# Two gate gemms, two norms and a split of the first block made one stage, with compact roots and output weights fetched ahead

## The reference, cut to what matters

```python
def rms_norm(t, w, groups):
    tg = t.reshape(t.shape[:-1] + (groups, t.shape[-1] // groups))
    tg = tg * lax.rsqrt(jnp.square(tg).mean(-1, keepdims=True) + EPS)
    return tg.reshape(t.shape) * w

def merge(s, y, o):   # z and g are columns of h @ w_in
    ys  = rms_norm(y * silu(s['z']), ssd_nw, 2)          # SSD_GROUPS = 2
    os_ = rms_norm(o, hg_nw, 8) * silu(s['g'])           # HG_HEADS = 8
    return jnp.concatenate([ys, os_], axis=-1) @ w_out
```

## Time and profile before

| | |
|---|---|
| runs | 3270.03, 3287.79, 3285.07 us |
| median | 3285.07 us |
| profiled execution, its own time | 3267.99 us |
| its span, first to last instruction | 3266.2 us |
| mean granted TensorE clock | 0.896 |
| TensorE (matmul) busy | 2748.4 us, 84% |
| VectorE busy | 1703.7 us, 52% |
| ScalarE busy | 1079.5 us, 33% |

### The profile page before, as it was taken

How to read it: one execution, slowest core, us unless ns; L and a number is a source line. 1 busy time by engine, 2 the same in 40 slices (tenths; PEclk the granted TensorE clock), 3 DMA queues, 4 the chain that set the end, 5 groups by cost and what they waited for, 6 DMA issues and landing times. The chain is left out here.

```text
span 3266.2 us, 41926 instructions
## 1 busy us (share of the span) xinstructions
PE 2748.4 (84%) x15966; PEld 2125.7 (65%) x15966; DVE 1703.7 (52%) x2643; ACT 1079.5 (33%) x1788; POOL 91.9 (3%) x101
## 2 busy tenths in 40 slices
PE   7979899756658999998968999957799847599998
PEld 4634887645346788786637888846666636478886
DVE  3535222677554588637976877342224362454432
ACT  3322101354212555324334554221124210245531
POOL 0034000000000000000000000000000000000000
PEclk9989999966878999999988999978769967699999
DMA  8723132001014233421112333222100100223332
GB/s 294 248 81 129 52 84 58 13 4 47 7 52 135 65 97 96 112 62 52 51 30 61 102 97 95 80 58 76 52 7 1 47 1 2 65 78 96 96 98 71
DMA packets 374147, 240.99 MB, mean 74 GB/s; under 512 B 8048, under 2 KB 345840, under 8 KB 374000
## 3 DMA queue, kind: packets, MB, share of 16 engines
q1 hardware_dynamic: 374000, 238.96, 24.6%
HBM read 236.31 MB, written 2.10 MB: 73 GB/s over the span
## 5 line engine op out<-in xcount | busy, mean ns | idle before, releaser
L1086 DVE SCALAR_TENSOR_TENSOR ffn_acc<-ffn_pad,cols_sb,ffn_acc 128x512 f32<-128x512 f32 x380 | 263.7, 746 | 32.6 <-ACT ffn_acc L1013 32.6
L223 PE MATMUL bank<-ffn_x_high,pre_high 128*128 128x512 f32 x528 | 212.2, 402 | 14.2 <-DVE ffn_x_low L475 10.7
L224 PE MATMUL bank<-ffn_x_low,pre_high 128*128 128x512 f32 x528 | 210.6, 399 | 0.0
L225 PE MATMUL bank<-ffn_x_high,pre_low 128*128 128x512 f32 x528 | 210.6, 399 | 0.0
L223 PE MATMUL bank<-ffn_x_high,ffn_w_high 128*128 128x512 f32 x528 | 205.5, 389 | 0.0
L225 PE MATMUL bank<-ffn_x_high,ffn_w_low 128*128 128x512 f32 x528 | 205.5, 389 | 0.0
L224 PE MATMUL bank<-ffn_x_low,ffn_w_high 128*128 128x512 f32 x528 | 205.4, 389 | 0.0
L223 PE MATMUL bank<-ffn_h_high,ffn_down_w_high 128*128 128x512 f32 x480 | 190.3, 397 | 0.0
L224 PE MATMUL bank<-ffn_h_low,ffn_down_w_high 128*128 128x512 f32 x480 | 189.6, 395 | 0.0
L225 PE MATMUL bank<-ffn_h_high,ffn_down_w_low 128*128 128x512 f32 x480 | 188.7, 393 | 0.0
L1307 DVE SCALAR_TENSOR_TENSOR conf_u<-conf_pad,cols_sb,conf_u 128x512 f32<-128x512 f32 x162 | 121.8, 752 | 16.9 <-ACT conf_u L1274 11.7
(11 more groups left out here) (734 smaller groups left out, 6388.0 us busy)
## 6 DMA issues: line engine op xcount, KB each, us to landing
ada_ring<-in_ada_w SPq DMA_DIRECT2D x48, 1024.0 KB, 7.0
pre_ring<-in_ffn_w_up SPq DMA_DIRECT2D x88, 512.0 KB, 3.9
pre_ring<-in_ffn_w_in SPq DMA_DIRECT2D x44, 512.0 KB, 3.9
ffn_down_ring<-in_ffn_w_down SPq DMA_DIRECT2D x28, 704.0 KB, 4.7
ffn_down_ring<-in_ffn_w_out SPq DMA_DIRECT2D x14, 704.0 KB, 4.5
pre_ring<-in_conf_w SPq DMA_DIRECT2D x18, 512.0 KB, 5.0
f_ring<-in_mix_w_in SPq DMA_DIRECT2D x32, 256.0 KB, 3.0
mix_out_ring<-in_mix_w_out SPq DMA_DIRECT2D x16, 512.0 KB, 3.9
```

Source lines behind the costliest of these rows:

```text
L223: pe.matmul(bank, weights[0], acts[0], start=start, stop=False)
L224: pe.matmul(bank, weights[0], acts[1], start=False, stop=False)
L225: return pe.matmul(bank, weights[1], acts[0], start=False, stop=stop)
L1086: dve.scalar_tensor_tensor(out=dst, in0=src, scalar=conv_w(2 * i + j, n), in1=dst, op0=ALU.mult, op1=ALU.add).then_inc(tapped[j], 1)
```

## The change

`gate_by`, `group_norm` and the call of `split` go. In their place stands one stage, `branch_gates`, that runs 16 gate tiles one after the other: tiles 0 to 7 are z's, tiles 8 to 15 are g's.

- Weight slabs come whole into the two slots of `pre_ring` and are split into `pre_high` and `pre_low` by ScalarE (`take_high`) and VectorE (`take_low`). Two more slabs, 16 and 17, are the weights of the output gemm's first tile; `closing` is told with `ahead=2 * DT` to take them from there.
- `o` is squared and counted ahead of the first product; `y` is squared and counted tile by tile. Roots are taken of 128 x 32 values (all of `o`) and 128 x 4 (a group of `y`) and spread over banks 5 and 6: for `o` two tiles at a time behind products 2 to 5, for the groups of `y` behind products 7 and 11.
- From tile 8 on VectorE forms `y` times gain and root, and `y` and the gated `o` are split in the same stage.

The diff, cut to its core:

```diff
-def gate_by(core, name, y, w_gate, x, sq=None):
...
-def group_norm(core, y, sq, groups, gain, square):
...
+def branch_gates(core, w_z, w_g, w_out, x, y, o, y_parts, o_parts):
...
+        o_counts, y_counts = banks[4], [banks[7], banks[4]]
...
+        def stage_at(s, shift=0):
+
+            return {1: 0, 6: 1, 10: 2}.get(s - shift)
+
+        @block.sync
+        def _(sp):
+            for s in range(slabs + 2):
+                if s >= 2:
+                    sp.wait_ge(low_done, s - 1)
+                sp.dma_start(ring[:, s % 2], slab(s)).then_inc(slab_in[s % 2], 16)
+
+        @block.tensor
+        def _(pe):
+            def product(s):
+                pe.wait_ge(low_done, s + 1)
+                if s >= 4:
+                    pe.wait_ge(gate_done, s - 3)
...
+            def o_root_out(k):
+                pe.wait_ge(inverted, 1)
+                if k >= 2:
+                    pe.wait_ge(o_scaled, k - 1)
+                spread_tokens(banks[5 + k % 2], lambda t: o_root[:, k * TT + t:k * TT + t + 1]).then_inc(o_spread, 1)
+
+            def y_root_out(n):
+                pe.wait_ge(inverted, n + 2)
+                pe.wait_ge(o_scaled, DT)
+                spread_tokens(banks[5 + n], lambda t: y_root[:, n, t:t + 1]).then_inc(y_spread, 1)
+
+            for k in range(DT):
+                o_count(k)
+            for s in range(slabs):
+                product(s)
+                if 2 <= s < 6:
+                    for k in range(2 * (s - 2), 2 * (s - 1)):
+                        o_root_out(k)
+                if 2 <= s < DT + 2:
+                    y_count(s - 2)
+                if s in (7, 11):
+                    y_root_out((s - 7) // 4)
+
+        @block.scalar
+        def _(act):
+            def take_high(s):
+                act.wait_ge(slab_in[s % 2], 16 * (s // 2 + 1))
+                if s >= 2:
+                    act.wait_ge(tile_done, s - 1)
+                act.activation(high[:, s % 2], ring[:, s % 2], ACT.Copy).then_inc(high_done, 1)
...
+            for k in range(DT):
+                if k >= 4:
+                    act.wait_ge(o_counted, k - 3)
+                act.activation(sq[:, k % 4, :], o[:, k, :], ACT.Square).then_inc(o_squared, 1)
+                if k in (3, 7):
+                    take_high(k // 4)
+            for s in range(slabs):
+                take_high(s + 2)
+                act.wait_ge(tile_done, s + 1)
+                if s >= 2:
+                    act.wait_ge(gated, s - 1)
+                act.activation(gate[:, s % 2, :], banks[s % 4][:, :], ACT.Silu).then_inc(gate_done, 1)
...
+                if stage_at(s) is not None:
+                    root(stage_at(s))
...
         @block.vector
         def _(dve):
...
+            take_low(0)
+            take_low(1)
+            for s in range(slabs):
+                take_low(s + 2)
+                if s >= DT:
+                    form_y(s - DT)
+                dve.wait_ge(gate_done, s + 1)
+                if s < DT:
+                    dve.tensor_tensor(y[:, s, :], y[:, s, :], gate[:, s % 2, :], ALU.mult).then_inc(gated, 1)
+                else:
+                    k = s - DT
+                    dve.wait_ge(o_scaled, k + 1)
+                    dve.tensor_tensor(o[:, k, :], o[:, k, :], gate[:, s % 2, :], ALU.mult).then_inc(gated, 1)
+                if stage_at(s) is not None:
+                    variance(stage_at(s))
+                if stage_at(s, 1) is not None:
+                    invert(stage_at(s, 1))
+                if 3 <= s < 7:
+                    for k in range(2 * (s - 3), 2 * (s - 2)):
+                        scale_o(k)
+                if s > DT:
+                    low_y(s - DT - 1)
+                if s > DT + 1:
+                    low_o(s - DT - 2)
+            low_y(DT - 1)
+            low_o(DT - 2)
+            low_o(DT - 1)
...
-        with core.room(branch_sq=[P, DT, SEQ]) as (sq,):
...
+        with core.split_room(y_parts=[P, DT, SEQ], o_parts=[P, DT, SEQ]) as (y_parts, o_parts):
+            branch_gates(core, w_in[:, MIX_AT["z"]:MIX_AT["xbc"]], w_in[:, MIX_AT["g"]:], w_out, h, y, o, y_parts, o_parts)
...
```

More of the change, by code:

```diff
@@ L2644, in _ @@
         @block.vector
         def _(dve):
[L2646 to L2677, removed]
+            def take_low(s):
+                dve.wait_ge(high_done, s + 1)
+                dve.tensor_tensor(low[:, s % 2], ring[:, s % 2], high[:, s % 2].bitcast(F32), ALU.subtract).then_inc(low_done, 1)
@@ new lines, in variance @@
+            def variance(n):
+                if n == 0:
+                    dve.wait_ge(o_counted, DT)
+                    dve.tensor_scalar(o_root[:, :], o_counts[:, 0:DT * TT], 1.0 / P, EPS, ALU.mult, ALU.add).then_inc(var_done, 1)
+                    return
+                dve.wait_ge(y_counted, per_group * n)
+                some = y_counts[n - 1][:, 0:per_group * TT].rearrange("p (k t) -> p t k", t=TT)
+                dve.tensor_reduce(y_root[:, n - 1, :], some, AX_X, ALU.add).then_inc(y_summed, 1)
+                dve.wait_ge(y_summed, n)
+                dve.tensor_scalar(y_root[:, n - 1, :], y_root[:, n - 1, :], 1.0 / (per_group * P), EPS, ALU.mult, ALU.add)\
+                   .then_inc(var_done, 1)
@@ new lines, in invert, with scale_o @@
+            def invert(n):
+                which = o_root[:, :] if n == 0 else y_root[:, n - 1, :]
+                dve.wait_ge(root_done, n + 1)
+                dve.reciprocal(which, which).then_inc(inverted, 1)
+            def scale_o(k):
+                dve.wait_ge(o_spread, k + 1)
+                dve.scalar_tensor_tensor(out=o[:, k, :], in0=o[:, k, :], scalar=core.col("hg_norm_w", k), in1=banks[5 + k % 2][:, :],
+                                         op0=ALU.mult, op1=ALU.mult).then_inc(o_scaled, 1)
@@ L2684, in even_mixer @@
         gla(core, w_in, h, h_ctx, o, const, ada)
-        with core.room(branch_sq=[P, DT, SEQ]) as (sq,):
[L2687 to L2695, removed]
+        with core.split_room(y_parts=[P, DT, SEQ], o_parts=[P, DT, SEQ]) as (y_parts, o_parts):
+            branch_gates(core, w_in[:, MIX_AT["z"]:MIX_AT["xbc"]], w_in[:, MIX_AT["g"]:], w_out, h, y, o, y_parts, o_parts)
+            closing(core, "mix_out", w_out, lambda k: [part[:, k % DT, :] for part in (y_parts, o_parts)[k // DT]], y, ahead=2 * DT,
+                    **close)
 HEAD_SCALE = HD ** -0.5
```

74 lines of the change are left out of this document (70 added, 4 removed).

## The result

| | before | after |
|---|---|---|
| Runs, us | 3286.4 median (3270.0 to 3302.7) | 3240.2 median (3237.5 to 3244.9) |
| Ratio of the runs | | 0.9874, 95% interval 0.9838 to 0.9909 |
| Profiled execution, its own time | 3268.0 | 3237.5 |
| First DMA of the stretch to first closing matmul | 797.20 to 993.32: 196.1 | 793.64 to 959.20: 165.6 |
| Closing gemm, first matmul to the next stage's first DMA | 103.0 | 104.0 |

The change makes the kernel faster by 1.3%. The two profiled executions differ by 30.5 us, and the stretch that the change rewrote accounts for 30.5 us: the prediction's 37.4 us came out 6.9 us too high. By this measure the kernel is 0.9% faster. (The stretch begins 3.6 us earlier after the change, and the closing gemm and the 2.2 ms behind it take that back.) The medians differ by 46 us, more than the stretch; the experiment without the prefetch shows why.

The account below looks back on a forecast made before the run. VectorE's reciprocals were taken to bound the norms; the new stage TensorE. Terms sum to 146.1 against 196.1 us: 50.0 saved, less 12.6 for clock, 37.4; 3268.0 becomes 3230.6, as a median 3247, range 3216 to 3265.

Parts of the forecast that it names:

- the clock behind the stalls: After each of six TensorE stalls, 3.5 us at the lower clock cost 1.4 us each, 8.4 us together.
- Start, counts of o at low clock included: Before the first product: 9.0 us for squares, the slab's cast and four remaining counts, plus 2.1 for low-clock counts.
- First product low: The first product starts at the low clock; 4.6 us of low level lose 2.1 us.
- 16 products: Gate products in the new stage follow one another every 5.60 us, 89.6 us, as before; slabs cost nothing.
- 10 spreads at high clock: Small f32 matmuls between products, 8 spreads for o and 2 for y, 1.1 us each: 11.0 us.
- Six stalls: TensorE idles behind products 2 to 5, 7 and 11, waiting for reciprocals or scalings on VectorE: 21.9 us together.
- Tail and between stages: After the last product: cast, low parts, forming and gate, 7.0 us, then 0.7 us to the next stage.
- rival of longer low stretches: Low clock lasts some 7 us after each stall, counts at upper bound: 26 us saved, 3259 us; chance 0.12.
- The counts at the start: Eight counts of o before the first product, at low clock 0.86 to 1.5 us each; 2.1 us extra taken.
- Table loads: ScalarE reloads its table seven times, four before, 1.28 us each; only three between a stalled TensorE and its reciprocal count.
- The closing gemm: Output gemm after the stage: the 6.3 us wait for its first weights goes; its 94.5 us stay.
- From profile to median: The profiled execution lay 17 us below the median of runs, so 3230.6 became 3247.7, predicted as 3247.

## Why the prediction was right, and where it was off

It said 3247 us within 3216 to 3265 and faster with 0.93; measured 3240. Forecast, sign and mechanism hold; one term, the clock behind the stalls, was sized too small. The stretch was to take 158.7 us, clock included; it took 165.6. Term by term, the measured value from the timeline of TensorE after:

| Term | predicted | measured | |
|---|---|---|---|
| Start, counts of o at low clock included | 11.1 | 14.4 | +3.3 |
| First product low | 2.1 | 1.6 | -0.5 |
| 16 products | 16 x 5.60 | 16 x 5.54 | -1.0 |
| 8 counts of y | 6.9 | 8 x 0.81 = 6.5 | -0.4 |
| 10 spreads at high clock | 11.0 | 8.9 | -2.1 |
| Six stalls | 21.9 | 22.6, and 0.16 each of a product's end | +1.7 |
| Clock behind the six | 8.4 | 14.6 | +6.2 |
| Tail and between stages | 7.7 | 7.7 | 0 |

They add up to +7.2 against the +6.9 measured.

*The order.* The stalls, which neither the diff nor a busy share shows, were predicted at their six places and within 0.25 us each. The experiments that move only the scalings, or only the reciprocals, remove exactly the ones named.

*The clock behind stalls* is the term that was mis-sized: "3.5 us of low level cost 1.4 us each". The length came from one row, where wide matmuls followed the gap at once, and it was taken for all six. Here the low level lasted 10.2 us at the first two stalls and 3.4 at the other four, and in it lay spreads and a count, which cost as much more as the products (pairs of spreads 3.4 to 3.8 us instead of 1.95). Against the same work at the high level, the timeline of TensorE gives 4.1 and 4.5 us lost behind the first two stalls and 1.3 to 1.5 behind each of the other four. So 1.4 us was right for four stalls and a third of the price for two. The first four together make 11.6 us by this count and 11.1 us by the experiment that filled them. The rival of longer low stretches had this mechanism; it was right for two stalls of six. Why two were long and four short is not settled. Length alone does not tell them apart: stalls of 3.82 us stand on both sides. The clock fell 1.8 and 1.0 us before TensorE went on in the two long ones, and in the other four at most 0.5 us before, or after it. The pattern came back in the kernel without the prefetch and in the one with the counts moved. But with the reciprocals moved it fell 0.6 us before the end of a stall of 3.82 us and stayed low for 10.2, so this does not decide it either.

*The counts at the start*: their price at the lower level "lies between 0.86 and 1.5 us", and 2.1 us in all was taken. They took 1.71 each (13.80 / 8 is 1.73), outside the bound: scaling by the slowdown of spreads was wrong, a count takes 1.8 times its 0.95 us. At that length the row, from 0.7 to 14.4 us of the stage, is itself the bound; that four counts would be done beside the squares and the first slab's way, and four be left, no longer mattered. The first product's low stretch was put at 4.6 us, a length that no row gives; it was 3.5.

*Table loads.* Seven, 1.28 us each; the silu starts 1.29 us behind the start of the load (827.39 to 828.68). The Trainium skill's 2.66 us for a switch (ScalarE: Activation LUTs, What ACT_TABLE_LOAD costs) is again not what this trace shows.

*The closing gemm* was to be unchanged; it took 104.0 us against 103.0. Its start is not the reason: the first 14 matmuls took 5.9 us at 0.50 after and 6.0 us before. Of the 1.0 us, 0.6 lie between the first matmul and the norm's first count, and 0.4 in the last spreads, which took 3.79 us in place of 3.38, with the clock low for longer around them; why is open. In the tail ahead of it, the prediction's 0.65 us for a low part stands in none of the rows that it names; in the timeline after they follow one another every 0.60 us.

*From profile to median.* 17 us were added since before's median lay so far above its profiled execution. That offset is the second group of runs, which, as far as the profiles tell, arises far behind the change and did not come up in the four runs after. Had they lain 20 us higher, the number would have been 13 us off in the other direction; that 3247 lies 7 from 3240 is in part luck: 6.9 us too much gain, and an offset of 17 where the four runs had 3.

## What to carry to other kernels

When work is interleaved into a stream of matmuls, write down for each wait of TensorE what stands ahead of the releasing instruction in its own engine's order; an instruction put behind the step's long wait releases a product later than it could. Moving scalings, reciprocals and four counts was worth 41.5 us here, more than the merging of stages with its prefetch (12.8). Price each stall with the clock that follows it (here 1.3 to 4.5 us, 2.8 in the mean of four, on top of 3.1 to 4.1). And keep one-column matmuls in small pieces between wide ones rather than in one long row: pieces of 16 records left the clock at 1.00 here, a row of 64 did not.

## What was not expected of the chip

- TensorE did not keep its clock although the profile has it fully busy (a matmul's end is modelled, and weight loads fill the same 7.50 of 7.50 us): in a row of 64 matmuls of one column it fell from 1.00 to 0.50 and stayed there until wide matmuls had come back. Counts ahead of the first product did not raise it either: it rose within product 0, 3.5 to 3.8 us after its start, whether 64 records of them preceded, 32 or none. The Trainium skill (TensorE: Matmul & The Clock Gate, Part 1) says that the chip does not count instructions and that, whatever is issued, work behind the first stretch of activity runs at the higher level. With one-column matmuls the row of 13.80 us at 0.53 does not agree, and the measurement decides.
- Unused matmuls of 512 columns in a stall held the clock at 1.00 and made the stretch 11.1 us shorter though none of their results is read.
- A piece 1.4 ms behind the closing gemm, the same instructions in every kernel here, ran at 1.00 in one profiled execution and at 0.53 in another, TensorE busy for 19.8 and 20.0 of 20.0 us, and what lies behind the closing gemm was 20.0 us apart in the two. That the two groups of times of one kernel come from it is likely, and not shown: only one execution of each kernel was profiled.
